# Projecting the eight sample tokens: contraction split, or output columns split, over TensorE's column groups

## The chip, the cores and the metric

One core of a Trainium2 chip runs the whole program. The metric is the device time of one execution in microseconds. TensorE (PE) multiplies, VectorE (DVE) and ScalarE (ACT) work elementwise and read PSUM, GpSimd (POOL) adds in SBUF, and SyncE (SP) issues most transfers. All data are fp32.

## The reference, cut to what matters

Two decoder layers over 512 prompt tokens and 8 sample tokens (one new token for each of 8 sequences). The part in question is the input projection, applied to both:

```python
def project_mixers(h, w_in_l, pos):          # h: rmsnorm(x, g_mix_pre[l]), 1024 wide
    z = h @ w_in_l
    qa, ka, va, qi, ki, wi, qb, kb, vb, gb = jnp.split(z, splits, axis=-1)
    ...                                      # rope on q, k, qi, ki
```

After it come a sparse attention (indexer scores, top-k, softmax over the selected keys), a retention mixer, an output product and a feed-forward block with squared ReLU.

## The kernel before

**Tiling.** The 520 tokens are five tiles: four of 128 prompt tokens (`NT` = 4) and tile 4 with the 8 sample tokens (`TILES` = 5, `NB` = 8). `w_in` is cut into eight chunks of columns, in the order indexer (324 columns, `W_IDX`), q, k, v of group A, q, k, gate, v of group B (512 each, `W`). `project(c, between)` (from L671) runs over the tiles of chunk `c`; the tile's number in the layer is n = 5c + i. For a prompt tile each of the eight contraction blocks k of 128 is one matmul (L690): 128 tokens stationary, 512 weight columns moving, added up in one PSUM bank. One fp32 matmul appears in the trace as two LDWEIGHTS and two MATMUL records.

**The sample tile before.** Eight tokens would fill 8 of the array's 128 columns. So the contraction is split: block k goes to the column group k // 2, that is to PSUM partitions 32(k // 2) and on (L694), with the last 32 tokens stationary, of which the last eight are wanted. The order of k is 0, 2, 4, 6, 1, 3, 5, 7, so that four column groups work side by side. Four partial sums then lie on four partition ranges. ScalarE copies the whole bank into `parts` (`take_parts`, L1155), and a matmul with the constant `addp` adds the four ranges up on partitions 0 to 7 of the same bank (`add_parts`, L649). TensorE issues that matmul after two blocks of the next tile. Then ScalarE scales and copies the result to SBUF (`evacuate`, L1182; in chunk 0 first the four columns of `wi`, L1178).

**What runs between.** `between(i, k)` is called after each block k and puts other work among the matmuls: transposes, indexer scores, and in chunks 4 (tile 3) to 6 the attention of 32 (block, head) steps (`attend`, steps listed by `head_steps`). A step's scores come from TensorE (L828), DVE masks them and takes the maximum (L1619, L1622), ScalarE exponentiates (L1221), DVE normalises (L1630), TensorE transposes (L838), ScalarE copies (L1216), TensorE multiplies with v (L815). Each engine has one order of work, written out by hand: ScalarE evacuates the tile before at the first step of a tile, and DVE ropes it (L1575 to L1581) or, for the gate, takes its sigmoid. Chunk 7 begins with the sample tile, with a group of transposes (L709) after every second block.

**Waits.** Two banks alternate (`proj_bank`, n % 2), so tile n waits until n - 2 is evacuated (`proj_read`, L680). In layer 0, chunk 0 is computed block by block for four prompt tiles in banks 0 to 3 (`first_chunk`, L659), after which TensorE waits for all constants (`const_in`, 13 loads on ScalarE's queue, the last is `addp`). The sample tile then uses bank 0 again. `token_sums`, `token_roots` and `token_scales` give each token's 1/rms, by which `evacuate` scales; for the sample tokens it is wanted on the partitions on which they are read. In layer 1 that runs inside chunk 0. SyncE's weight loads wait for `proj_done` of the chunk that used the ring slot.

Of the kernel before, what the change touches and what calls it, by code (L numbers as in the profile page):

```python
# [23 lines left out]
NB = 8  # L24
# [25 lines left out]
CONSTS = 13  # L50
# [14 lines left out]
def token_cols(t):  # L65
    return slice(t * P, t * P + rows(t))

# [119 lines left out]
def down_ready(q, which):  # L187
# [8 lines left out]
    proj_done=40, tok_mm=2, part_mm=8, tr_mm=19, ts_mm=3, dot_mm=12, sdot_mm=1, wm_mm=1, ssc_mm=1, cache_used=16,  # L196
    vrep_mm=1, spt_mm=1, att_mm=32, pt_mm=32, pv_mm=32, as_mm=1, ra_mm=8, su_mm=4, o_mm=4, bt_mm=5, mt_done=16,
    stat_mm=6, st_mm=168, tok_std=3, proj_read=40, part_read=8, tr_read=19, ts_read=3, dot_read=12, srelu_done=1,
# [42 lines left out]
def build(nc, x, w_idx, w_all, gains, g_first, g_ret, cache_k, cache_v, cache_ki, state, pages, tab_cos, tab_sin,  # L241
# [3 lines left out]
    with ctx:  # L245
# [95 lines left out]
        parts = sb("parts", [P, W]); addp = sb("addp", [P, NB]); dg = sb("dg", [P, NH]); ones = sb("ones", [P, P]); eps = sb("eps", [P, 1])  # L341
# [34 lines left out]
        part_mm = sem("part_mm")  # L376
        part_read = sem("part_read")
# [103 lines left out]
        def proj_bank(n):  # L481
            return n if now[0] == 0 and n < NT else n % 2
# [130 lines left out]
        def _(pe):  # L613
# [30 lines left out]
            def add_parts(n):  # L644

                c = n // TILES
                pe.wait_ge(part_read, past(part_read) + c + 1)
                width = W if c else W_IDX
                mm(ps[0:NB, proj_bank(n), 0:width], addp[:], parts[:, 0:width], start=True, stop=True).then_inc(proj_done, 1)  # L649
# [19 lines left out]
            def project(c, between):  # L669
                width = W if c else W_IDX  # L670
                for i, t in enumerate(tile_order(c)):  # L671
# [11 lines left out]
                    for j, k in enumerate(ks):  # L683
                        if i == 0 and j == (4 if t < NT else 2):
                            unit_here(2 * c + 1)
# [394 lines left out]
        def _(act):  # L1080
# [213 lines left out]
            for l in range(DEPTH):  # L1294
# [54 lines left out]
                for g in range(2):  # L1349
                    if g:  # L1350
                        take_parts(3)
# [887 lines left out]
```

## Time and profile before

| | |
|---|---|
| median of 3 runs | 1653.7 us (1651.63 to 1654.96) |
| the profiled execution | 1654.42 us, its span 1652.6 us |
| TensorE, matmul records | 1580.8 us, 96% of the span, 6986 records |
| TensorE, weight loads | 1101.5 us, 67% |
| DVE, ScalarE, GpSimd | 831.6 us (50%), 432.5 us (26%), 420.8 us (25%) |
| DMA | 150.26 MB, mean 91 GB/s |
| granted TensorE clock | 0.987 of 2.4 GHz, mean |

Layer 0 goes to about 824 us; the projection and its mixers take the stretch to about 365 us in layer 0, and 824 to about 1180 us in layer 1. The output products and the feed-forward block fill the rest. A matmul record counts as busy to its modelled end, also while the next one runs beside it, so a high share does not mean that the array works at its peak. Idle time stands beside a group with what ended it.

### The profile page before, as it was taken

How to read it: one execution, taken by the hardware profiler on the slowest of the kernel's cores; microseconds unless marked ns; L12 is line 12 of the kernel's file. 1: busy time of each engine (PE TensorE's matmuls, PEld its weight loads, DVE VectorE, ACT ScalarE, POOL GpSimd, SP SyncE). 2: the span in 40 equal slices, each digit the busy share in tenths (PEclk: the TensorE clock that was granted, in tenths of full speed). 3: DMA queues.
4: the chain of work that ended last, by engine and by line, in shares of the span. 5: the costliest groups of instructions: out<-in, count | busy, mean ns of one | idle time of the engine just before them, and what ended most of it. 6: DMA issues, size and time to landing. Idle time of an engine off the chain costs nothing.

```text
span 1652.6 us, 19575 instructions
## 1 busy us (share of the span) xinstructions
PE 1580.8 (96%) x6986; PEld 1101.5 (67%) x6986; DVE 831.6 (50%) x1761; ACT 432.5 (26%) x975; POOL 420.8 (25%) x332
## 2 busy tenths in 40 slices
PE   7999899999999999999989998999999999999995
PEld 4344344478888888888843433445888888888884
DVE  4498556684743002332566984577646420133335
ACT  4312244314422002210142212443244310032100
POOL 0000000113363433353420000010226433343451
PEclk9999999999999999999999999999999999999998
DMA  6135401121422122312123252101233312222211
GB/s 203 63 127 167 146 20 52 53 78 55 153 102 103 72 82 102 103 51 102 63 94 102 77 202 105 52 1 54 81 103 127 105 74 103 102 80 100 77 51 52
DMA packets 52498, 150.26 MB, mean 91 GB/s; under 512 B 8331, under 2 KB 29331, under 8 KB 39091
## 3 DMA queue, kind: packets, MB, share of 16 engines
q1 hardware_dynamic: 44770, 140.65, 24.3%
q10 hardware_dynamic: 7632, 8.36, 1.5%
q8 instruction: 56, 0.92, 0.2%
q14 instruction: 40, 0.32, 0.1%
HBM read 139.79 MB, written 9.02 MB: 90 GB/s over the span
## 4 chain that ended last, share of the span: by engine, by line
PE 76%; DVE 16%; ACT 3%; issue 2%; DMA 2%; SPq 1%; ACTq 0%; DVEq 0%; POOL 0%; POOLq 0%
PE ps L1028 42%; PE ps L690 17%; PE ps L966 7%; DVE arena L1604 1%; DVE x_feat L1753 1%; DVE top L1602 1%; DVE arena L1643 1%; PE ps L694 1%; PE ps L828 1%; ACT arena L1182 1%; DVE s_sb L1751 1%; PE ps L815 1%; PE ps L838 1%; PE ps L649 1%; PE ps L924 1%
## 5 line engine op out<-in xcount | busy, mean ns | idle before, releaser
L690 PE MATMUL ps<-wring,h_feat 128*128 128x512 f32 (+1 forms) x960 | 438.6, 596 | 4.2 <-ACT arena L1182 2.8
L690 PEld LDWEIGHTS ps<-wring,h_feat 128*128 128x128 f32 x960 | 173.3, 193 | 192.7 <-issue 181.2
L1028 PE MATMUL ps<-arena,wring 128*128 128x256 f32 (+1 forms) x1280 | 285.8, 382 | 0.3 <-DVE arena L1832 0.3
L1028 PEld LDWEIGHTS ps<-arena,wring 128*128 128x128 f32 x1280 | 243.1, 190 | 37.7 <-DVE arena L1832 1.1
L1028 PE MATMUL ps<-h_feat,wring 128*128 128x256 f32 (+1 forms) x768 | 176.8, 382 | 2.5 <-DVE arena L1832 2.5
L2086 POOL TENSOR_TENSOR wring<-wring,arena 128x512 f32<-128x512 f32 (+1 forms) x48 | 78.8, 1641 | 341.2 <-PE ps L1028 321.6
L1028 PEld LDWEIGHTS ps<-h_feat,wring 128*128 128x128 f32 x768 | 145.8, 190 | 24.8 <-DVE arena L1832 3.3
L1028 PE MATMUL ps<-mix,wring 128*128 128x256 f32 (+1 forms) x512 | 123.6, 391 | 3.9 <-DVE s_sb L1806 3.9
L1028 PE MATMUL ps<-arena 128*128 128x264 f32 x512 | 119.2, 386 | 0.0
L966 PE MATMUL ps<-mix,wring 128*128 128x256 f32 (+1 forms) x512 | 115.0, 383 | 0.8 <-ACT mix L1242 0.8
L1028 PEld LDWEIGHTS ps<-mix,wring 128*128 128x128 f32 x512 | 99.4, 194 | 20.9 <-DVE s_sb L1806 4.8
L2069 POOL TENSOR_TENSOR pt_sb<-pt_sb 128x256 f32<-128x256 f32 (+1 forms) x98 | 76.7, 783 | 130.7 <-ACT pt_sb L1114 127.7
L1028 PEld LDWEIGHTS ps<-arena 128*128 128x128 f32 x512 | 97.3, 190 | 16.4
L966 PEld LDWEIGHTS ps<-mix,wring 128*128 128x128 f32 x512 | 96.5, 190 | 15.5 <-issue 1.2
L1182 ACT ACTIVATE arena<-ps,rtok 128x512 f32<-128x512 f32 (+3 forms) x80 | 53.2, 665 | 201.1 <-PE ps L690 173.0
L2110 POOL TENSOR_TENSOR arena<-arena,gret 128x512 f32<-128x512 f32 (+1 forms) x10 | 14.6, 1458 | 320.6 <-ACT arena L1189 320.6
L2086 POOL TENSOR_TENSOR arena<-wring 128x512 f32<-128x512 f32 (+1 forms) x48 | 79.0, 1646 | 50.5 <-DMA wring<-in_w_all 33.1
L1283 ACT ACTIVATE arena<-arena 128x264 f32<-128x264 f32 (+1 forms) x96 | 40.4, 421 | 192.4 <-DVE arena L1832 143.5
L2086 POOL TENSOR_TENSOR wring<-wring 128x512 f32<-128x512 f32 (+1 forms) x48 | 79.0, 1645 | 3.8
L2086 POOL TENSOR_TENSOR arena<-arena,wring 128x512 f32<-128x512 f32 (+1 forms) x48 | 78.9, 1643 | 3.8
L2104 POOL COPY arena<-kTs 128x4 f32<-128x4 f32 x16 | 3.1, 191 | 245.9 <-ACT kTs L1343 229.1
L1028 PE MATMUL ps<-h_feat,arena 128*128 128x264 f32 x256 | 62.2, 386 | 0.0
(212 smaller groups left out, 1800.8 us busy)
## 6 DMA issues: line engine op xcount, KB each, us to landing
wring<-in_w_all SPq DMA_DIRECT2D x108, 1024.0 KB, 5.0
arena<-in_cache_k SPq DMA_DIRECT2D x32, 256.0 KB, 5.3
arena<-in_cache_v SPq DMA_DIRECT2D x32, 256.0 KB, 4.3
wring<-in_w_idx SPq DMA_DIRECT2D x4, 648.0 KB, 5.6
x_feat<-in_x SPq DMA_DIRECT2D x4, 520.0 KB, 6.4
o_k_out<-arena ACTq DMA_DIRECT2D x2, 1024.0 KB
o_v_out<-arena ACTq DMA_DIRECT2D x2, 1024.0 KB
arena<-in_state SPq DMA_DIRECT2D x2, 1024.0 KB, 4.9
```

What stands on the lines that cost most here:

```text
L649: mm(ps[0:NB, proj_bank(n), 0:width], addp[:], parts[:, 0:width], start=True, stop=True).then_inc(proj_done, 1)
L690: last = mm(ps[:, proj_bank(n), 0:width], h_feat[:, k, token_cols(t)], wt, start=(k == 0), stop=(k == KD - 1))
L694: last = mm(ps[q4:q4 + 32, proj_bank(n), 0:width], h_feat[:, k, TOK - 32:TOK], wt, start=(k % 2 == 0), stop=(k % 2 == 1))
L815: last = mm(ps[e * HD:(e + 1) * HD, 6 + b % 2, (h // 2) * P:(h // 2 + 1) * P], v_tok[:, m, (h + e) * HD:(h + e + 1) * HD], pt_sb[e][:, m * ...
L828: mm(ps[:, 4 + e, 0:(b + 1) * P], qT[rr, h // 2, b * P:(b + 1) * P], kT[rr, h // 2, 0:(b + 1) * P], start=True, stop=True).then_inc(att_mm, 1)
L838: last = nc.tensor.transpose(ps[:, 2 + j % 2, m * P:(m + 1) * P], p_sb[j % 2][:, m * P:(m + 1) * P], idn[:])
L966: last = mm(ps[:, item_bank(n), 0:span(h)], wring[u % SLOTS][:, (m % 2 * KD + k) * P:(m % 2 * KD + k + 1) * P], mix[:, k, HALVES[h]], star ...
L1028: last = mm(out, a[:, j, :], b, start=(opens(n) and j == 0), stop=(j == nk - 1), skip_group_check=True)
L1182: nc.scalar.activation(dst, src, ACT.Copy, scale=rtok[0:r, sc, t:t + 1]).then_inc(proj_read, 1)
L1283: nc.scalar.activation(f, f, ACT.Relu).then_inc(act_step, 1)
L2069: nc.gpsimd.tensor_tensor(ssum[:, hc], ssum[:, hc], sqr[added % 2][:, 0:span(h)], ALU.add).then_inc(sq_used, 1)
L2086: nc.gpsimd.tensor_tensor(dst, in0, in1, op).then_inc(s_ready, 1)
```

## The change

The sample tile's output columns, not its contraction, are spread over the column groups. For each block k four matmuls, one per group g, multiply the same 8 tokens (stationary, 8 columns) with a quarter of the weight columns (128; in chunk 0 80, 80, 80 and 84). Group g's result lies complete on partitions 32g to 32g + 7. There are 32 small matmuls per tile in place of 8, in the plain order of k. `take_parts`, `add_parts`, their two semaphores, the tensors `parts` and `addp` and the load of `addp` go. `evacuate` reads the four pieces one after another from their partitions and joins them in SBUF; in chunk 0 the last is preceded by `wi`. The scales of the sample tokens are computed on four partition ranges: `token_sums(1)` makes four small matmuls for them and `token_roots(1)` four roots. In layer 0, the sample tile of chunk 0 gets bank 4 and waits for no evacuation, and the two tiles after it wait for two.

```diff
+def sample_cols(c):
+    cuts = (0, 80, 160, 240, W_IDX) if c == 0 else (0, P, 2 * P, 3 * P, W)
+    return list(zip(cuts[:-1], cuts[1:]))
...
         def proj_bank(n):
-            return n if now[0] == 0 and n < NT else n % 2
+            return n if now[0] == 0 and n < TILES else n % 2
+        def bank_taken(n):
+            if now[0] == 0 and n < TILES:
+                return None
+            return past(proj_read) + (2 if now[0] == 0 and n in (TILES, TILES + 1) else n - 1)
...
             def token_sums(h):
-                for t in ((0, 1), (2, 3, NT))[h]:
-                    last = mm(ps[0:rows(t), 6 + h, t:t + 1], ssum[:, token_cols(t)], ones[:, 0:1], start=True, stop=True)
+                for t in ((0, 1), (2, 3))[h]:
+                    last = mm(ps[:, 6 + h, t:t + 1], ssum[:, token_cols(t)], ones[:, 0:1], start=True, stop=True)
+                for q4 in range(0, P if h else 0, 32):
+                    last = mm(ps[q4:q4 + NB, 6 + h, NT:TILES], ssum[:, SEQ:TOK], ones[:, 0:1], start=True, stop=True)
...
-                    if n == NT and now[0] == 0:
-                        pe.wait_ge(proj_read, 1)
-                    elif n >= 2:
-                        pe.wait_ge(proj_read, past(proj_read) + n - 1)
-                    ks = range(KD) if t < NT else (0, 2, 4, 6, 1, 3, 5, 7)
+                    if n >= 2 and bank_taken(n):
+                        pe.wait_ge(proj_read, bank_taken(n))
...
                         else:
-                            q4 = 32 * (k // 2)
-                            last = mm(ps[q4:q4 + 32, proj_bank(n), 0:width], h_feat[:, k, TOK - 32:TOK], wt,
-                                      start=(k % 2 == 0), stop=(k % 2 == 1))
-                        if j == 1 and n and (i == 0 or tile_order(c)[i - 1] == NT):
-                            add_parts(n - 1)
+                            for g, (c0, c1) in enumerate(sample_cols(c)):
+                                last = mm(ps[32 * g:32 * g + NB, proj_bank(n), 0:c1 - c0], h_feat[:, k, SEQ:TOK], wt[:, c0:c1],
+                                          start=(k == 0), stop=(k == KD - 1))
...
+                    for q4 in range(0, P, 32):
+                        rr = slice(q4, q4 + NB)
+                        nc.scalar.activation(std_tok[rr, NT:TILES], ps[rr, 7, NT:TILES], ACT.Sqrt, bias=eps[rr]).then_inc(tok_std, 1)
...
-                if t == NT and counts.get(part_read.num, 0) == past(part_read) + c:
-                    take_parts(c)
...
+                pieces = sample_cols(c) if t == NT else [(0, W if c else W_IDX)]
+                for g, (c0, c1) in enumerate(pieces):
+                    rr, end = slice(32 * g, 32 * g + r), (W if c else W_IDX - NI)
+                    if c1 > end:
...
+                    done = proj_read if g == len(pieces) - 1 else act_step
+                    nc.scalar.activation(dst[:, c0:c1], ps[rr, proj_bank(n), 0:c1 - c0], ACT.Copy,
+                                         scale=rtok[rr, sc, t:t + 1]).then_inc(done, 1)
+                    act.wait_ge(done, up(done))
```

## Rows read from the trace of the kernel before

**Rows 1.** The profile page, chain that ended last, shares by engine.

```profile
PE 76%; DVE 16%; ACT 3%; issue 2%; DMA 2%; SPq 1%; ACTq 0%; DVEq 0%; POOL 0%; POOLq 0%
```

**Rows 2.** Busy time by stretch: PE, PEld, DVE, ACT, POOL (instructions), clock, DMA share, GB/s.

```profile
45.60:189.00 143.40, 137.91 (x487) 56.55 (x486) 104.22 (x249) 30.80 (x58) 1.53 (x8) 0.99 0.38 126
189.00:311.00 122.00, 112.17 (x536) 50.31 (x536) 78.03 (x211) 52.81 (x125) 7.29 (x5) 0.99 0.13 47
```

**Rows 3.** Groups by form, whole span: count, busy us, mean ns, idle before.

```profile
L694 PE MATMUL ps<-wring,h_feat 128*32 128x512 f32 x224 | 32.7, 602 | 0.0
L649 PE MATMUL ps<-parts,addp 128*8 128x512 f32 x28 | 14.6, 604 | 9.9 <-ACT parts L1155 9.9
...
L1182 ACT ACTIVATE arena<-ps,rtok 8x512 f32<-8x512 f32 x14 | 9.5, 677 | 14.5 <-PE ps L649 14.3
L1155 ACT ACTIVATE parts<-ps 128x512 f32<-128x512 f32 x14 | 8.4, 597 | 5.2 <-PE ps L694 4.9
...
L1216 ACT ACTIVATE pt_sb<-ps 128x128 f32<-128x128 f32 x16 | 4.4, 277 | 18.8 <-PE ps L838 17.8 <-ACT p_sb L1221 0.9
```

**Rows 4.** Small passes, loads and two waits of TensorE's sequencer: timeline, groups, lines.

```profile
280.24 1.09 PE L815 MATMUL ps<-pt_sb,arena 128*64 128x128 f32 x16
...
136.88 1.95 PE L797 MATMUL ps<-arena,qs 128*32 128x257 f32 x32
...
193.67 0.16 PEld L694 LDWEIGHTS ps<-wring,h_feat 128*32 128x32 f32 x8
...
L649 PEld LDWEIGHTS ps<-parts,addp 128*8 128x8 f32 x32 | 1.7, 87 | 22.1 <-ACT parts L1155 16.8 <-issue 5.3
...
L792 PEldq EVENT_SEMAPHORE  x1: 51/51/51, 150.7 to 150.7; - x1
...
L680 PEldq EVENT_SEMAPHORE  x1: 51/51/51, 151.3 to 151.3; - x1
```

**Rows 5.** Timeline of the start of layer 0: start, length, what, idle before and releaser.

```profile
29.02 1.28 ACT L1130 ACT_TABLE_LOAD   x1 [13.93 <-DMA addp<-in_sum_parts]
...
32.28 2.39 PE L694 MATMUL ps<-wring,h_feat 128*32 128x324 f32 x16 [4.19 <-ACT arena L1182]
...
32.46 0.53 ACT L1182 ACTIVATE arena<-ps,rtok 128x320 f32<-128x320 f32 x1
...
40.53 0.48 DVE L1581 TENSOR_TENSOR arena<-arena,rstd_ffn 8x320 f32<-8x320 f32 x1
...
43.14 1.04 PE L709 MATMUL ps<-idn,arena 128*128 128x128 f32 x8
```

**Rows 6.** Timeline at the change from chunk 4 to chunk 5, layer 0.

```profile
199.80 0.29 DVE L1630 TENSOR_SCALAR p_sb<-p_sb,rinv 128x128 f32<-128x128 f32 x1
...
200.84 1.03 PE L649 MATMUL ps<-parts,addp 128*8 128x512 f32 x2 [2.08 <-ACT parts L1155]
...
204.74 0.68 DVE L1575 TENSOR_TENSOR arena<-arena,cosT 8x512 f32<-8x512 f32 x1 [3.60 <-ACT arena L1182]
```

**Rows 7.** Chunk 5 to 6, layer 0: timeline, and the stretch behind the adding matmul.

```profile
249.62 1.03 PE L649 MATMUL ps<-parts,addp 128*8 128x512 f32 x2 [2.61 <-ACT parts L1155]
...
250.60:252.50 1.90, 1.90 (x5) 0.40 (x4) 0.00 (x0) 0.00 (x0) 0.00 (x0) 0.53 0.40 78
...
255.07 0.56 DVE L1619 CUSTOM_DVE_ANT_0 s_sb<-ps,arena 128x384 f32<-128x384 f32 x1 [6.28 <-PE ps L828]
```

**Rows 8.** Timeline of the first tile of chunk 7, layer 0.

```profile
306.70 1.05 PE L694 MATMUL ps<-wring,h_feat 128*32 128x512 f32 x4
...
308.28 1.23 ACT L1203 ACTIVATE arena<-ps 128x512 f32<-128x512 f32 x2
```

**Rows 9.** Timeline of layer 1: the token scales in chunk 0, and chunk 3's adding matmul.

```profile
848.05 0.24 ACT L1133 ACTIVATE std_tok<-ps,eps 8x1 f32<-8x1 f32 x1
849.15 0.26 ACT L1178 ACTIVATE wi<-ps,rtok 128x4 f32<-128x4 f32 x1 [0.85 <-PE ps L690]
...
969.61 1.02 PE L649 MATMUL ps<-parts,addp 128*8 128x512 f32 x2 [0.49 <-ACT parts L1155]
```

More of the change, by code:

```diff
@@ L49 @@
 CHUNKS = 8
-CONSTS = 13
+CONSTS = 12
 FT = 16
@@ L340, in build @@
         idn = sb("idn", [P, P]); exps = sb("exps", [NB, 2, P]); sel = sb("sel", [P, 2, NB])
-        parts = sb("parts", [P, W]); addp = sb("addp", [P, NB]); dg = sb("dg", [P, NH]); ones = sb("ones", [P, P]); eps = sb("eps", [P, 1])
+        dg = sb("dg", [P, NH]); ones = sb("ones", [P, P]); eps = sb("eps", [P, 1])
         pg = sb("pg", [1, NB * NPAGES], I32)
@@ L676, in project @@
                         unit_here(2 * c)
-                    if n == NT and now[0] == 0:
-                        pe.wait_ge(proj_read, 1)
-                    elif n >= 2:
-                        pe.wait_ge(proj_read, past(proj_read) + n - 1)
-                    ks = range(KD) if t < NT else (0, 2, 4, 6, 1, 3, 5, 7)
-                    for j, k in enumerate(ks):
-                        if i == 0 and j == (4 if t < NT else 2):
+                    if n >= 2 and bank_taken(n):
+                        pe.wait_ge(proj_read, bank_taken(n))
+                    for k in range(KD):
+                        if i == 0 and k == 4:
                             unit_here(2 * c + 1)
@@ L692, in project @@
                         else:
-                            q4 = 32 * (k // 2)
-                            last = mm(ps[q4:q4 + 32, proj_bank(n), 0:width], h_feat[:, k, TOK - 32:TOK], wt,
-                                      start=(k % 2 == 0), stop=(k % 2 == 1))
-                        if j == 1 and n and (i == 0 or tile_order(c)[i - 1] == NT):
-                            add_parts(n - 1)
-                        if j < KD - 1:
-                            between(i, j)
-                    last.then_inc(proj_done if t < NT else part_mm, 1)
+                            for g, (c0, c1) in enumerate(sample_cols(c)):
+                                last = mm(ps[32 * g:32 * g + NB, proj_bank(n), 0:c1 - c0], h_feat[:, k, SEQ:TOK], wt[:, c0:c1],
+                                          start=(k == 0), stop=(k == KD - 1))
+                        if k < KD - 1:
+                            between(i, k)
+                    last.then_inc(proj_done, 1)
                     between(i, KD - 1)
@@ L1094, in _ @@
                      (causal_bias[:], causal), (sel[:], select), (dg[:], diag), (dm[:], dmask), (kdec[:], k_decay),
-                     (qdec[:], q_decay), (cdec[:], c_decay), (gam[:], s_gamma), (addp[:], sum_parts)]
+                     (qdec[:], q_decay), (cdec[:], c_decay), (gam[:], s_gamma)]
             assert len(loads) == CONSTS
@@ L1149, in normed @@
                 square(norm, h, k, x_feat[:, k, HALVES[h]])
-            def take_parts(c):
-                n, width = c * TILES + tile_order(c).index(NT), W if c else W_IDX
-                act.wait_ge(part_mm, past(part_mm) + c + 1)
-                nc.scalar.activation(parts[:, 0:width], ps[:, proj_bank(n), 0:width], ACT.Copy).then_inc(part_read, 1)
-                act.wait_ge(part_read, up(part_read))
             def evacuate(c, i):
@@ L1383, in _ @@
                 take_groups([qT[:, h, :] for h in range(4)])
-                take_parts(7)
                 take_groups([kT[:, h, :] for h in range(4)])
@@ L1856, in token_scales @@
             def token_scales(h):
-                dve.wait_ge(tok_std, past(tok_std) + (3 if h else 1))
+                dve.wait_ge(tok_std, past(tok_std) + (6 if h else 1))
                 ts = slice(2, TILES) if h else slice(0, 2)
```

26 lines of the change are left out of this document (5 added, 21 removed).

## Prediction

> **What bounds the kernel now.** I read the chain of waits first, then the busy time by stage, then the groups by form, then the order of events around each adding matmul. The chain [rows 1] lies on TensorE for 76% of the span, VectorE for 16% and ScalarE for 3%: what TensorE issues, and what it waits for, sets the end. The stages differ [rows 2]. In chunks 1 to 4 (45.6 to 189 us) TensorE is busy for 137.9 of 143.4 us; in the attention stretch (189 to 311) for 112.2 of 122, with the other engines far from full, so three engines hand work around and the missing 10 us are waits. The product and feed-forward stages behind are not touched.
>
> The profiled execution took 1654.4 us, of which the span is 1652.6. The median is 1653.7, so I make the sum against 1654.4 and take nothing off for the 0.7.
>
> **Sample tiles.** One fp32 matmul shows as two MATMUL records, "passes". Before, a sample tile is 16 passes of 512 columns. 224 such records fill 32.7 us although each lasts 0.60 [rows 3], so four column groups run beside each other, and a tile is four rounds, about 1.85 us. After, it is 64 passes of 128 columns on the same four groups, the same columns per group: 16 rounds of four passes. How long is a round? Two-group matmuls of 128 columns put 16 passes, eight rounds of two, into 1.09 us [rows 4]. That holds the drain of the last; without a drain of some 0.2 a round is 0.11 us, a quarter of the 0.43 that a round of 512 columns takes: the columns alone. Sixteen rounds give 1.75 us: as long as before, within 0.1. Two things could make a round longer. The weight loads: a load of 8 columns is recorded with 87 ns, but eight loads of 32 columns at 193.67 lie within 0.16 us [rows 4], each 0.11 long, so they start some 7 ns apart and overlap. And the sequencer: after a blocked wait at 150.7 (L792) it reaches the wait behind sixteen such matmuls (L680) at 151.3 [rows 4], 0.6 us for 32 passes and 32 loads, under 40 ns a matmul; the new tile needs one per 54 ns. I take 0.03 us more per tile, 0.5 us in all; the bounds are 0 and what the first rival costs.
>
> The Trainium skill ("TensorE: Matmul & The Clock Gate", Part 1) says that with hardware decode off the sequencer spends about 62 ns per MATMUL. By that rule 64 passes last 3.97 us a tile and the sum below would come out at about 1661 us; the 32 passes in 0.6 us speak against it here, though they are the only such place I found.
>
> **Adding matmuls.** They go: 28 records of 512 columns in 14.6 us and 9.9 us of idle in front of them [rows 3], 0.955 us of TensorE each from start to next start, 0.64 in chunk 0. TensorE is the bound in chunks 1 to 3, so three times 0.955 = 2.9 us come back in each layer. DVE is full from 79 to 151 us, but it starts that run on the sample tile's evacuation, which also comes earlier, so it keeps pace. In chunk 3 of layer 1 there is also 0.49 us of idle in front [rows 9]: 0.4 more.
>
> **Evacuation.** ScalarE lost a copy of 0.60 us per tile and now makes four pieces in place of one of 0.68 [rows 3]. A 128-column copy takes 0.28 [rows 3], with a semaphore step about 0.31, so four pieces are 1.2 to 1.3 us: 0.6 more on the way from the tile's last matmul to the rope, against 1.6 (copy, adding matmul) taken out of it. Where DVE or TensorE waits for that rope this 0.6 counts, and it is in the terms below. Elsewhere ScalarE waits for TensorE and hides it. If that cover were gone everywhere it would cost 16 x 0.6 = 10 us. SyncE's weight loads wait for the end of a chunk's last tile, which comes earlier; no queue is moved past another.
>
> **Start of layer 0.** The sample tile waited for bank 0 until 32.28 (4.19 idle) and the stage's transposes began at 43.14 [rows 5]. Now the tile has bank 4 and can run as soon as the constants are in (29.0), and the next tile waits for two evacuations (33.0) [rows 5] where it waited for four. It ends at about 40, 16 passes of 0.43 later; its transposes then wait for the last rope, L1581 ending at 41.0 [rows 5], which does not move: ropes are late next. That is 2.1 us, and 0.3 more since ScalarE, which evacuated tile 5 before it took the transposes' first group, has done so by then: 2.4. ScalarE's first work, at 29.02, was released by the DMA of addp, the last constant [rows 5]; without it that comes between 0 and 1 us earlier (TensorE's own first stage ends at 28.1); I take 0.3. Together 2.7 (0.6 to 3.7).
>
> **Chunk 4 to 5.** TensorE stood 2.08 us for the copied parts at 200.84, before 0.955 us of adding [rows 6]: 3.0 at most. But the next steps hang on DVE, which idled 3.60 us until the sample tile was evacuated and started its rope at 204.74 [rows 6]. Without the adding matmul ScalarE still has step 5's copy and exponential behind DVE's L1630 of 199.80; they end near 201.4, four pieces end near 202.7, the rope starts at 202.8. So 2.0 (0.96 to 3.0) per layer.
>
> **Chunk 5 to 6.** The same with 2.61 us of wait [rows 7], and worse: the two passes behind it fill 1.9 us at a granted clock of 0.53 in that stretch (near the 1.2 GHz level), after the engine had stood, against 0.86 at the full one. Step 20's score matmuls stood behind all that, and DVE idled 6.28 us for them [rows 7]. So TensorE gains 2.6, 0.95 and 1.0 for the clock up to step 20, and 0.6 in that step, which ran half slow too: 5.2. DVE's rope of the sample tile gains the same less the 0.6 of the pieces: 4.6. DVE and TensorE wait for each other by turns behind it; I take 5.0 (0.96 to 5.2) per layer.
>
> **Chunk 6 to 7.** Two adding matmuls, 1.9 us. Also, chunk 7 begins with the sample tile, cut by transposes after each two k; of the four column groups such a pair used two, and its four passes took 1.05 us with the drain [rows 8], 0.98 to the next start. Now a pair of k fills all four groups: four rounds, 0.44. Four times 0.54 gives 2.2. But the third transpose group waits until ScalarE has taken the first, which it began at 308.28 [rows 8]; without the wait for the adding matmul, and with the pieces, that is near 307.1, its end 307.7, and TensorE is there at 306.8: it stands 1.0 us where it stood none. Net 1.9 + 2.2 - 1.0 = 3.1 (1.9 to 4.1).
>
> **Layer 1, chunk 0.** The adding matmul gives 0.64. The deviation of the sample tokens is now wanted on four partition ranges: four small matmuls, and three more ScalarE roots of 0.24 [rows 9] that overlap a little, in front of the scales for which L1178 at 849.15 waits [rows 9]. That is 0.65 later. Net 0 (-0.3 to 0.3).
>
> **Sum.** Layer 0: 2.7 + 2.9 + 2.0 + 5.0 + 3.1 = 15.7. Layer 1: 0 + 3.3 + 2.0 + 5.0 + 3.1 = 13.4. Less 0.5 for the tiles: 28.6. 1654.4 - 28.6 = 1625.8, say **1626 us**; with the terms' bounds 1618 to 1634.
>
> **Rivals.** First, *the small passes do not fit in a round*. If the 1.95 us that 32 passes of 257 columns took [rows 4] is a rate of 60 ns a pass rather than their columns, a tile lasts 3.84 us, 2.1 more, sixteen times 33.6: 1626 + 33.6 = 1659 us, slower. At the recorded 87 ns of an 8-column load [rows 4], 5.57 us a tile, it would be near 1685. It decides from 1.8 us more per tile, 55 ns a pass, on. For it: these passes come one in some 54 to 60 ns and I found no long stretch with faster ones, and that is break-even. Against: in all of them the columns explain that number, and the loads and the sequencer go faster [rows 4]. Chance 0.12.
>
> Second, *the attention stretch keeps its length*: softmax steps on DVE and ScalarE take the place of the waits for the copied parts. Then the 14 us of chunk 4 to 6 shrink to about 2: 1638 to 1640. For it: DVE's steps form a chain there and DVE starts at once where it can. Against: its idle of 3.60 and 6.28 us sits exactly behind these waits. Chance 0.2.
>
> Third, *partial gain*: rounds of 0.14 us in place of 0.11 (0.5 us a tile) and a longer evacuation, 1634. Chance 0.08. The forecast has 0.6.
>
> **Range.** 1618 to 1643: forecast, third and second rival and their edges; only the first lies outside. A difference of 0.2%, 3.3 us, is about what a measurement of this kernel can tell from none. Only the first rival reaches that side: faster 0.87, same 0.05 (a first rival at break-even), slower 0.08.
>
> **What would show it.** Sample tile of chunk 1: start to next start near 1.8 us (first rival: over 3). No idle over 1 us at the two places where it was 2.08 and 2.61; the rope of the sample tile of chunk 4 some 2 us, the scores of step 20 some 5 us nearer to the tile before them. Start: transposes near 41.0. Chunk 7: pairs of k at 0.44 to 0.5. If tiles stay at 1.8 and the gain is small, the prediction fails in the attention stretch; if they are long, in the round.

## The result and the profile after

The kernel after takes 1628.4 us (median of 4 runs, 1627.58 to 1632.61) against 1652.66 us for the kernel before beside it (4 runs, 1651.55 to 1654.96): a ratio of 0.9857, 95% interval 0.9836 to 0.9878. Measured again on another chip it was 1628.85 against 1653.92, ratio 0.9850 (0.9835 to 0.9864). The forecast was 1626, the range 1618 to 1643. Where a gain stands below with an interval, both are worked out from the ratio; the difference of the medians can be 1.6 us off it.

First the page of the profiled run (1627.84 us, span 1626.1): busy time, and the chain that ended last by engine, to be read against [rows 1].

```profile
PE 1557.1 (96%) x7734; PEld 1116.2 (69%) x7734; DVE 832.8 (51%) x1761; ACT 438.3 (27%) x1013; POOL 421.4 (26%) x332
...
PE 69%; DVE 20%; ACT 5%; issue 3%; DMA 2%; POOL 1%; SPq 0%; ACTq 0%; DVEq 0%; POOLq 0%
```

TensorE's share of the chain fell from 76% to 69%, VectorE's rose from 16% to 20% and ScalarE's from 3% to 5%. The hand-overs between engines weigh more now; that is where the rest of this document finds what was mis-sized.

The groups of TensorE by form (busy us, mean ns, idle in front), which answer to [rows 3], then ScalarE's:

```profile
L696 PE MATMUL ps<-wring,h_feat 128*8 128x128 f32 x896 | 29.3, 273 | 0.0
...
L1178 ACT ACTIVATE arena<-ps,rtok 8x128 f32<-8x128 f32 x56 | 20.2, 361 | 6.3 <-PE ps L696 4.6
```

896 small passes fill 29.3 us. A piece of the evacuation takes 361 ns, where the forecast had 0.28 from a plain copy of 128 columns [rows 3].

The timeline of TensorE around the sample tile of chunk 1, layer 0 (start, length, what):

```profile
72.73 1.94 PE L696 MATMUL ps<-wring,h_feat 128*8 128x128 f32 x64
74.59 1.98 PE L692 MATMUL ps<-wring,h_feat 128*128 128x512 f32 x4
```

From start to next start it is 1.86 us for 64 passes. The tile is as long as before, and no adding matmul cuts the next one. That saves more than the adding matmul's 0.955 us: before, the next tile's first eight passes took 1.92 us ahead of the cut (75.48 to 77.40) and 1.92 behind it (78.35 to 80.27); uncut they take 3.64 (74.59 to 78.23), 0.2 less.

The start of layer 0, TensorE and ScalarE, which answers to [rows 5]:

```profile
29.21 1.82 PE L696 MATMUL ps<-wring,h_feat 128*8 128x80 f32 x64 [2.47 <-DMA gam<-in_s_gamma]
33.75 8.59 PE L692 MATMUL ps<-wring,h_feat 128*128 128x512 f32 x16 [2.72 <-ACT arena L1178]
42.18 1.04 PE L709 MATMUL ps<-idn,arena 128*128 128x128 f32 x8
...
29.23 1.28 ACT L1130 ACT_TABLE_LOAD   x1 [14.51 <-DMA gam<-in_s_gamma]
...
30.83 1.07 ACT L1135 ACTIVATE std_tok<-ps,eps 8x1 f32<-8x1 f32 x4
```

And the granted clock there (window, length, busy by engine, PEclk, DMA share, GB/s):

```profile
33.00:36.00 3.00, 2.25 (x3) 1.17 (x4) 2.76 (x8) 2.16 (x6) 0.00 (x0) 0.50 1.00 421
36.00:42.00 6.00, 6.00 (x14) 2.57 (x13) 5.38 (x14) 1.55 (x5) 0.00 (x0) 0.94 0.27 115
```

Chunk 4 to 5 of layer 0 ([rows 6] before), TensorE, then VectorE's rope of the sample tile and ScalarE's pieces:

```profile
199.15 2.10 PE L883 MATMUL ps<-sel,arena 128*128 128x8 f32 x16
201.11 3.39 PE L692 MATMUL ps<-wring,h_feat 128*128 128x512 f32 x4
...
195.59 0.68 DVE L1567 TENSOR_TENSOR arena<-arena,cosT 8x512 f32<-8x512 f32 x1 [1.91 <-ACT arena L1178]
...
193.96 1.54 ACT L1178 ACTIVATE arena<-ps,rtok 8x128 f32<-8x128 f32 x4
```

Chunk 5 to 6 ([rows 7] before) and chunk 7 ([rows 8]):

```profile
237.57 2.81 PE L692 MATMUL ps<-wring,h_feat 128*128 128x512 f32 x6 [0.52 <-ACT arena L1178]
240.32 0.88 PE L815 MATMUL ps<-pt_sb,arena 128*64 128x128 f32 x12
...
292.18 0.62 PE L696 MATMUL ps<-wring,h_feat 128*8 128x128 f32 x16
292.74 0.66 PE L709 MATMUL ps<-idn,arena 128*128 128x128 f32 x4
...
295.86 0.66 PE L709 MATMUL ps<-idn,arena 128*128 128x128 f32 x4 [0.77 <-ACT arena L1200]
```

Where the stall of 2.61 us was, 0.52 is left. A pair of k of chunk 7 takes 0.56 us to the next start.

Chunk 3 of layer 1 ([rows 9] has its adding matmul), TensorE, then ScalarE:

```profile
953.22 2.06 PE L852 MATMUL ps<-arena,exps 8*128 8x512 f32 x4 [0.77 <-ACT arena L1178]
955.21 5.24 PE L692 MATMUL ps<-wring,h_feat 128*128 128x512 f32 x8
...
949.04 1.28 ACT L1348 ACT_TABLE_LOAD   x1 [4.83 <-DVE nms L1909]
...
951.53 1.54 ACT L1178 ACTIVATE arena<-ps,rtok 8x128 f32<-8x128 f32 x4
```

To see where the time went, take the start of the same matmul in both traces. This table is worked out from them (us; "gain" is before less after; tuned2 is a kernel of the last experiment):

```
same matmul                                    before    after   gain   tuned2
first transposes of layer 0                     43.14    42.18    1.0    42.17
2nd tile of chunk 2, layer 0                    85.08    83.04    2.0    82.75
2nd tile of chunk 3, layer 0                   119.14   115.95    3.2   115.66
scores of the cache (L870), layer 0            182.82   175.09    7.7   174.20
step behind chunk 4 to 5 (L828), layer 0       212.29   204.80    7.5   201.14
step behind chunk 5 to 6, 2nd tile             262.01   249.88   12.1   245.44
behind chunk 7 (L894), layer 0                 319.42   304.49   14.9   299.88
chunk 0 of layer 1, 1st tile                   828.81   812.64   16.2   808.24
2nd tile of chunk 1, layer 1                   901.00   883.76   17.2   879.55
2nd tile of chunk 2, layer 1                   935.05   916.67   18.4   912.74
2nd tile of chunk 4, layer 1                   997.51   980.12   17.4   975.88
step behind chunk 4 to 5, layer 1             1025.13  1006.01   19.1  1000.96
step behind chunk 5 to 6, layer 1             1074.85  1051.08   23.8  1045.26
behind chunk 7's groups, layer 1              1128.73  1102.15   26.6  1096.15
```

Each column is one profiled run, so single places carry chance. A second profiled run of the kernel after (on the other chip) has 4.7 in place of 7.7 at L870 of layer 0 and 25.4 in place of 26.6 in the last row; between the rows behind chunk 4 to 5 and those behind chunk 5 to 6 it has the same 4.7 in both layers.

### The profile page after: what moved, and what is told of

Read it like the earlier page. It is cut to its first block, busy times and chain, and to the rows that moved or that the text cites. A ratio compares the mean times of both kernels' runs of the same rounds, so it can differ in the third digit from the quotient of the medians.

```text
span 1626.1 us, 21092 instructions
## 1 busy us (share of the span) xinstructions
PE 1557.1 (96%) x7734; PEld 1116.2 (69%) x7734; DVE 832.8 (51%) x1761; ACT 438.3 (27%) x1013; POOL 421.4 (26%) x332
## 4 chain that ended last, share of the span: by engine, by line
PE 69%; DVE 20%; ACT 5%; issue 3%; DMA 2%; POOL 1%; SPq 0%; ACTq 0%; DVEq 0%; POOLq 0%
PE ps L1028 43%; PE ps L692 12%; PE ps L966 6%; DVE arena L1596 3%; DVE top L1594 3%; ACT arena L1178 2%; DVE x_feat L1745 1%; DVE arena L1635 1%; DVE arena L1567 1%; DVE arena L1573 1%; PE ps L828 1%; DVE s_sb L1743 1%; DVE s_sb L1611 1%; PE ps L924 1%; PE ps L838 1%
## 5 line engine op out<-in xcount | busy, mean ns | idle before, releaser
L692 PE MATMUL ps<-wring,h_feat 128*128 128x512 f32 (+1 forms) x960 | 436.2, 595 | 7.5 <-ACT arena L1178 6.0
L692 PEld LDWEIGHTS ps<-wring,h_feat 128*128 128x128 f32 x960 | 174.9, 193 | 188.6 <-issue 176.4
L1178 ACT ACTIVATE arena<-ps,rtok 128x512 f32<-128x512 f32 (+3 forms) x128 | 65.5, 512 | 194.2 <-PE ps L692 185.2
L1028 PE MATMUL ps<-mix,arena 128*128 128x264 f32 x256 | 62.2, 386 | 0.0
```

The source lines that it names most:

```text
L692: last = mm(ps[:, proj_bank(n), 0:width], h_feat[:, k, token_cols(t)], wt, start=(k == 0), stop=(k == KD - 1))
L1028: last = mm(out, a[:, j, :], b, start=(opens(n) and j == 0), stop=(j == nk - 1), skip_group_check=True)
L1178: nc.scalar.activation(dst[:, c0:c1], ps[rr, proj_bank(n), 0:c1 - c0], ACT.Copy, scale=rtok[rr, sc, t:t + 1]).then_inc(done, 1)
```

## Experiments

The times of before are 1653.07 us (20 runs) beside the three parts alone and the part undone; 1652.4 (13) beside the cut passes, the one piece, the later adding matmul and the first tuning; 1653.92 (9) beside the last two kernels; and 1652.67 (9) beside the one of chunks 4 and 5 with the later adding matmul.

**One part alone: chunks 4 and 5 (run cols45).** In this and the next two kernels the copy and the adding matmul stay for the chunks named.

```diff
+CONTRACTED = (0, 1, 2, 3, 6, 7)
...
+                    whole = t < NT or c not in CONTRACTED
...
+                        elif not whole:
+                            q4 = 32 * (k // 2)
+                            last = mm(ps[q4:q4 + 32, proj_bank(n), 0:width], h_feat[:, k, TOK - 32:TOK], wt,
...
+                            if tile_order(pc)[pi] == NT and pc in CONTRACTED:
+                                add_parts(n - 1)
```

> The kernel before, with the sample tile split by columns in chunks 4 and 5 alone; the other six chunks keep contraction parts, copy and adding matmul. Theory (the waits for the copied parts are what costs, as the forecast had it): 2.0 + 5.0 us per layer, 14.0 in all, so 1638.6; going by where the kernel after gained, 0.2 to 1.7 us at chunk 4 to 5 and 4.6 at chunk 5 to 6 in each layer, it is 11 us, about 1641.5. Rival (only the adding matmuls count, other waits of the attention stretch take the place of the two stalls): 4 x 0.955 = 3.8 us, about 1649.

Measured: 1644.07 us, ratio 0.9936 (0.9915 to 0.9957), 10.6 us less with an interval of 7 to 14. (The medians differ by 9.0.) By the rows of the table above, the trace gives 4.6 us at chunk 5 to 6 in both layers. Chunk 4 to 5 gains 1.7 us up to L883 in both layers and gives 1.6 back on the way to the step behind, in slow passes. The rival of 3.8 us falls. The same trace gains 2.6 us in chunk 3 of layer 0, where this kernel changes nothing: so much can come and go there by chance.

**One part alone: chunks 1 to 3 (run cols123).** `CONTRACTED = (0, 4, 5, 6, 7)`.

> The kernel before, with the split by columns in chunks 1, 2 and 3 alone. Theory (TensorE is the bound there): 2.9 us in layer 0 and 3.3 in layer 1 by the forecast, about 1646.5. By the trace of the kernel after, 1.15 us per chunk in chunks 1 and 2 of each layer, 1 to 3 in chunk 3 of layer 0, where the transfers of the cache end the wait, and a loss of up to 0.8 in chunk 3 of layer 1: 5.5 to 7.5 us, 1645 to 1647. Rival (VectorE, which is full behind chunk 1, keeps the length): under 2 us, 1651 or more.

Measured: 1648.73 us, 0.9970 (0.9954 to 0.9986): 5.0 us less, interval 2.3 to 7.6. In layer 1 the three chunks gain 1.14, 1.14 and 0.96 us in the trace. TensorE is the bound there, and a chunk gives 1.15, not 0.955: the adding matmul and the 0.2 of the cut. TensorE's row at the end of chunk 3, layer 1:

```profile
965.33 1.95 PE L871 MATMUL ps<-arena,exps 8*128 8x512 f32 x4 [0.64 <-ACT arena L1208]
967.21 3.70 PE L703 MATMUL ps<-wring,h_feat 128*128 128x512 f32 x8
```

Nearly the stall of the kernel after (0.77), but the eight passes behind it take 3.70 us and not 5.24. So of what chunk 3 of layer 1 lost in the kernel after, 1.5 us is clock, not the change's order.

This kernel also has the old order at chunk 5 to 6, with the old stall, and happens to keep its clock there:

```profile
247.74 1.02 PE L664 MATMUL ps<-parts,addp 128*8 128x512 f32 x2 [2.61 <-ACT parts L1178]
248.70 1.12 PE L703 MATMUL ps<-wring,h_feat 128*128 128x512 f32 x2
```

The two passes behind it take 1.05 us to the next start where the kernel before took 1.90 [rows 7], and the place is 1.6 us shorter in both layers with nothing changed in it. So of what a kernel without slow passes saves there against the profiled run of before, 1.6 us is clock. The slow passes of this run lie at chunk 4 to 5 of layer 0 instead, which is 2.0 us longer, also unchanged.

**One part alone: chunk 7 (run cols7).** `CONTRACTED = (0, 1, 2, 3, 4, 5, 6)`.

> The kernel before, with the split by columns in chunk 7 alone, where the sample tile comes first and is cut by transposes after each two k. Theory: the adding matmul of chunk 7 goes (0.955), a pair of k goes from 0.98 to 0.55 us to the next start (four times 0.43 = 1.7), and the third group of transposes stands up to 0.8 us for ScalarE: 1.9 to 2.7 us per layer, about 1648.5 in all. Rival (only the adding matmul counts, and the pairs of k are hidden behind ScalarE's taking of the groups): 2 x 0.955 less the wait, 1652 or so.

Measured: 1649.23 us, 0.9980 (0.9970 to 0.9991): 3.3 us less, interval 1.5 to 5.0. The trace gives 1.9 us per layer in chunk 7, in two parts: 0.8 up to the first full tile and 1.1 at the transposes behind it. The theory holds, the rival (1652) lies outside.

The three parts alone sum to 10.6 + 5.0 + 3.3 = 18.9 us of the 24.3. Chunks 0 and 6 were not run alone; the trace of the kernel after has about 1 us for the start and 0.9 per layer for chunk 6's adding matmul (2.8 at chunk 6 to 7, less the 1.9 of chunk 7), and the rest is within the scatter of the clock.

**One part undone: the bank and the early tile (run bank0).**

```diff
-            return n if now[0] == 0 and n < TILES else n % 2
+            return n if now[0] == 0 and n < NT else n % 2
-            return past(proj_read) + (2 if now[0] == 0 and n in (TILES, TILES + 1) else n - 1)
+            return past(proj_read) + n - 1
```

> The kernel after, with one part undone: in layer 0 the sample tile of chunk 0 again goes to bank 0 and waits for the first evacuation, and the next tile waits for four. The forecast's term for the early tile was 2.4 us (2.7 with the constants): then this kernel is 2.4 us slower than the kernel after, 1630.8. Theory from the trace of the kernel after, where chunk 1's first tile starts early only to run 8.6 us at a low granted clock: the early tile brings 0.5 us or less, 1628 to 1629, and chunk 1's first tile runs at a higher granted clock than in the kernel after.

Measured: 1632.01 us, 0.9868 (0.9844 to 0.9892), 3.6 us over the kernel after; the intervals overlap. The profiled run is 8.8 us longer than after's in its span, and its mean granted clock is 0.984 against 0.989. Two stretches of it:

```profile
34.73 9.65 PE L692 MATMUL ps<-wring,h_feat 128*128 128x512 f32 x16 [1.31 <-ACT arena L1178]
...
156.00:163.00 7.00, 7.00 (x10) 2.66 (x9) 6.69 (x14) 1.20 (x2) 0.00 (x0) 0.52 1.04 394
```

My expectation that the tile behind would run at a higher clock fell: it takes 9.65 us. The times alone hardly tell what the bank is worth: two of the four runs, at a clock of 0.989, took 1629.7 and 1630.3, 0.7 to 2.4 us more than the kernel after at that clock. The traces tell more. Counted from the last constant (28.27 here, 29.23 in the kernel after), chunk 1's first tile starts after 6.46 us here and after 4.52 in the kernel after, and 4.51 to 4.52 in three more profiled runs with bank 4 (the second of the kernel after, the cut passes, the one piece). That is 1.9 us for the early tile, so the theory's 0.5 falls. The first transposes follow after 15.9 us here and 13.0 to 14.5 in those four, so the forecast's 2.4 is in reach; the tile between runs through the slow clock in each of them and adds the scatter.

**The price of a pass (run halves).** Each sample matmul of 128 columns cut in two.

```diff
-                            for g, (c0, c1) in enumerate(sample_cols(c)):
+                            for part in range(2 if c else 1):
+                                for g, (c0, c1) in enumerate(sample_cols(c)):
+                                    h0, h1 = (part * (P // 2), (part + 1) * (P // 2)) if c else (0, c1 - c0)
```

> The kernel after, with each sample matmul of 128 columns in chunks 1 to 7 cut into two of 64 (128 passes a tile in place of 64, the same columns; chunk 0 as it was). Theory (the columns set the tile, what the sequencer and the weight loads need per pass lies under them): no change, 1628 us, and a tile of 1.9 us from start to next start. First rival of the forecast (a pass costs what it costs, whatever its columns), with its price lowered to the 29 ns a pass that the kernel after shows at most (64 passes in 1.86 us): 1.86 us more per tile, 14 tiles, 26 us more, 1654. Anything between tells the true price of a pass.

Measured: 1630.7 us, 0.9873 (0.9850 to 0.9896). TensorE in chunk 1:

```profile
72.32 1.97 PE L698 MATMUL ps<-wring,h_feat 128*8 128x64 f32 x128
74.22 1.98 PE L692 MATMUL ps<-wring,h_feat 128*128 128x512 f32 x4
```

128 passes from start to next start in 1.90 us, 15 ns a pass; the tile grew by 0.04. The columns set the tile, and the first rival is out by far. (This kernel leaves something out: the sample rows of chunks 1 to 7 are not the full sums. Both halves start in one bank, and the later start seems to make the first half lose its first k, which was not tried by itself. The work issued is as described.)

**The price of four pieces (run one_piece).**

```diff
-                pieces = sample_cols(c) if t == NT else [(0, W if c else W_IDX)]
+                pieces = sample_cols(c) if t == NT and c == 0 else [(0, W if c else W_IDX)]
```

> The kernel after, with the sample tile of chunks 1 to 7 evacuated by one ScalarE copy of 512 columns from the first partition range, as in the kernel before. It leaves out three of the four pieces of these tiles (what is copied is right in the first 128 columns alone). Theory: four pieces take 1.54 us where one takes 0.68, and this counts where VectorE or TensorE waits for the evacuation: at chunk 4 to 5 and 5 to 6 of each layer about 0.8 us each, at chunk 3 of layer 1 up to 0.8, in chunk 7 up to 0.8 per layer: 3 to 5 us less than the kernel after, 1624 to 1625. Rival (ScalarE is hidden everywhere): no change, 1628.

Measured: 1616.71 us, 0.9791 (0.9774 to 0.9808), 11.7 us under the kernel after, two to four times what the theory had. The same place as above, ScalarE, VectorE and TensorE:

```profile
193.27 0.68 ACT L1178 ACTIVATE arena<-ps,rtok 8x512 f32<-8x512 f32 x1
...
194.05 0.68 DVE L1567 TENSOR_TENSOR arena<-arena,cosT 8x512 f32<-8x512 f32 x1 [1.04 <-ACT arena L1178]
...
199.35 1.96 PE L692 MATMUL ps<-wring,h_feat 128*128 128x512 f32 x4
```

Four pieces take 1.54, one takes 0.68: the difference of 0.86 appears whole at each of eight places, at chunk 3, 4 to 5, 5 to 6 and 6 to 7 of both layers (by the starts of the same matmuls 0.8 to 1.1 each; 0.7 of it is given back in layer 0 at the cache's transfers). That is some 7 us. The rest is the clock: `L692` x4 takes 1.96 in place of 3.39, chunk 3 of layer 1 has no stall and no slow passes behind it (2.5 us in all), and the mean clock of the four runs is 0.991 to 0.993, that of the nine runs of the kernel after 0.987 to 0.990.

**The place of the adding matmul (run late3).** The kernel before, one number changed.

```diff
-                        if j == 1 and n and (i == 0 or tile_order(c)[i - 1] == NT):
+                        if j == 3 and n and (i == 0 or tile_order(c)[i - 1] == NT):
```

> The kernel before, with the adding matmul issued after the fourth k of the next tile in place of the second, 0.86 us later in the order of TensorE. The two stalls of TensorE, 2.08 and 2.61 us, shrink by that to 1.2 and 1.7, while the copied parts and so the evacuation and the rope come no earlier. Theory (in the attention stretch the way copy, adding matmul, evacuation, rope sets the time, TensorE's own standing little): within 1 us of the kernel before. Rival (what TensorE stands is lost one for one): 4 x 0.86 = 3.4 us less, 1649.6.

Measured: 1647.46 us, 0.9971 (0.9959 to 0.9983), 4.8 us less (2.8 to 6.8). My theory fell, and the rival is too small at the decisive place. By the trace this kernel gains 4.3 us at chunk 5 to 6 in both layers, nearly the 4.6 of the kernel after, and 1.4 at chunk 4 to 5. It gives back 1.7 us in chunk 3 of layer 0 and 4.8 in layer 1, there 3.0 of it in slow passes. TensorE at chunk 5 to 6:

```profile
244.85 2.81 PE L690 MATMUL ps<-wring,h_feat 128*128 128x512 f32 x6 [0.52 <-ACT arena L1182]
247.60 0.88 PE L815 MATMUL ps<-pt_sb,arena 128*64 128x128 f32 x12
248.40 0.92 PE L828 MATMUL ps<-arena 64*128 64x384 f32 x4
...
250.59 1.02 PE L649 MATMUL ps<-parts,addp 128*8 128x512 f32 x2
```

The head step's matmuls (L815, L828) need nothing of the copied parts. Before, they stood behind the blocked adding matmul; here they run first, and when the adding matmul comes its parts are ready. It costs 0.95 and no stall. Of the 4.3 us, 2.7 are the stall and 1.6 the clock, which was low behind the stall in both layers of the profiled run of before (see the run of chunks 1 to 3).

**The place alone, where it helps (run late45).** The same edit for chunks 4 and 5 only.

```diff
-                        if j == 1 and n and (i == 0 or tile_order(c)[i - 1] == NT):
+                        if j == (3 if c in (5, 6) else 1) and n and (i == 0 or tile_order(c)[i - 1] == NT):
```

> The kernel before, contraction parts, copies and adding matmuls all kept; only the adding matmuls of chunks 4 and 5 are issued two k of the next tile later, behind the head step's matmuls, as in the run late3, and those of the other chunks stay where they were. Theory (what costs at chunk 4 to 5 and 5 to 6 is that TensorE waits for the copied parts in front of a head step that does not need them, the matmul itself counts 0.955 at most): by the places in late3 1.4 + 4.6 us per layer, some 12 us less the 1 to 1.5 us that come back in chunk 7: 1642 to 1645, as much as the split by columns in the same two chunks gave (1644). Rival (only taking out copy and adding matmul brings it; what late3 showed there was the clock): 1649 or more.

Measured: 1640.62 us, 0.9921 (0.9907 to 0.9936), 13.1 us less (10.6 to 15.4), against 10.6 (7 to 14) for the split by columns in the same two chunks. The trace has the same 1.4 and 4.3 us per layer as late3, 11.3 in all, and nothing back in chunk 7. The split by columns has 1.7 and 4.6 there where no slow pass takes it back, so the two edits are within 0.6 us per layer of each other, and the lead of 2.5 us of this one lies in the clock (0.991 to 0.992 against 0.988 to 0.991). So most of what these chunks had to give does not hang on taking the adding matmul out. It hangs on what stands behind it in TensorE's queue, and one changed line brings it.

**A first tuning of the new costs (run tuned).**

```diff
                     token_roots(0)
-                    token_roots(1)
                     for i in range(2):
                         evacuate(0, i)
+                    token_roots(1)
...
-                    nc.scalar.activation(std_tok[:, 2:NT], ps[:, 7, 2:NT], ACT.Sqrt, bias=eps[:]).then_inc(tok_std, 1)
-                    for q4 in range(0, P, 32):
+                    nc.scalar.activation(std_tok[:, 2:TILES], ps[:, 7, 2:TILES], ACT.Sqrt, bias=eps[:]).then_inc(tok_std, 1)
...
+                    if g >= len(pieces) - 2:
+                        act.wait_ge(done, count)
```

> The kernel after, with three edits where its trace shows the new costs. In layer 0 ScalarE evacuates the first two tiles ahead of the second set of roots (as layer 1 does); the deviations of the third and fourth tile and of the sample tokens are one root over all partitions in place of five, with one matmul that fills the rows between the samples; ScalarE no longer waits after each of the four pieces, only ahead of the last. Theory: the next tile of chunk 1 in layer 0 starts near 32 in place of 33.75 and the ropes 1 us earlier, 1.0 us; four roots are 0.7 to 0.8 us of ScalarE in layer 1 too, of which up to 0.6 counts; four pieces take 1.3 us in place of 1.54, which counts at five or six places with 0.2: 2 to 3 us less than the kernel after, 1625.5. Rival (these waits are hidden, or the granted clock takes it back): 1628.

Measured: 1628.87 us, 0.9870 (0.9851 to 0.9889), nothing gained. The next tile started at 32.5 in place of 33.75, but ran through the same slow clock, and the first transposes came at 41.96 in place of 42.18; four pieces took 1.52 in place of 1.54, so the waits between them had cost next to nothing. The ropes came no earlier either: the second set of scales now stands behind two ropes in VectorE's order, ScalarE waited 3.10 us for it, and the last rope ended at 41.91 in place of 41.61. The mean clock of these runs was 0.9875. The rival was right.

**The kernel after once more (run after2), and a version with the eight places mended (run tuned2).** The edits of tuned2 beside those of the start:

```diff
+                if t == NT and c in SHARED:
+                    dve.wait_ge(proj_done, past(proj_done) + n + 1)
+                    for g, (c0, c1) in list(enumerate(sample_cols(c)))[2:]:
+                        v.tensor_scalar(raw[(j * TILES + t) % 3][0:NB, c0:c1], ps[rr, proj_bank(n), 0:c1 - c0],
...
                 for g in range(2):
+                    if g:
+                        evacuate(3, 4)
...
-                evacuate(6, TILES - 1)
                 block_out(NT - 1)
-                take_groups([qT[:, h, :] for h in range(4)])
+                take_groups([qT[:, h, :] for h in range(2)])
+                evacuate(6, TILES - 1)
+                take_groups([qT[:, h, :] for h in range(2, 4)])
```

> The kernel after once more, beside tuned2 on the same chip. Both theories: 1628 us, within 3.

> The kernel after, with edits at the four places where the run with one piece gained: (1) chunks 4 and 5: VectorE, which waits there, takes the third and fourth piece of the sample tile while ScalarE takes the first two; (2) chunk 3: ScalarE evacuates the sample tile between its two softmax exponentials in place of behind both; (3) chunk 6: ScalarE writes the last attention output and takes the first two groups of transposes ahead of the sample tile's pieces; (4) the start as in the tuned kernel: roots in one, two evacuations ahead of the second set. All the work is there. Theory (the four pieces lie on the way of VectorE and TensorE at these places): 0.7 to 0.8 us each at chunk 3, 4 to 5, 5 to 6 and 6 to 7 of both layers, about 6 us, and one or two stretches of low granted clock less, 1.5 us each: 1620 to 1622. Rival (the run with one piece gained by what it leaves out of the rows' data or by the clock alone): 1626 or more.

Measured: the kernel after 1628.85 us, 0.9850 (0.9835 to 0.9864); tuned2 1618.06 us, 0.9787 (0.9773 to 0.9800), 10.8 us under it, with all the work in. VectorE and ScalarE share the pieces at chunk 4 to 5, and chunk 3 of layer 1 has no stall:

```profile
192.54 0.73 DVE L1573 TENSOR_SCALAR arena<-ps,rtok 8x128 f32<-8x128 f32 x2
193.63 0.68 DVE L1585 TENSOR_TENSOR arena<-arena,cosT 8x512 f32<-8x512 f32 x1 [0.35 <-ACT arena L1183]
...
192.78 0.75 ACT L1183 ACTIVATE arena<-ps,rtok 8x128 f32<-8x128 f32 x2
...
948.47 1.98 PE L858 MATMUL ps<-arena,exps 8*128 8x512 f32 x4
950.38 3.70 PE L698 MATMUL ps<-wring,h_feat 128*128 128x512 f32 x8
```

The rival falls. By the starts of the same matmuls the places give 0.35 us at chunk 3 of layer 0 and 0.8 to 1.05 at each of the other seven, 6.4 in all, as the theory had it; the rest of the 10.8 goes with the clock (mean 0.991 to 0.993, the kernel after 0.987 to 0.990). It is the fastest kernel here that does the whole work. It was not run without the edits at the start; by the run before they bring nothing.

## Why the prediction was right

The sum was 28.6 us; the profiled run is 26.6 shorter (1654.4 to 1627.8), the median 24.3. The mechanism was right, and the near agreement also hides errors that cancel. Part of it is luck: the start and the evacuation were sized wrong, and in the one trace of before chunk 3 of layer 0 and a later stage ran slow by chance, which made up for it. The terms' bounds, all low or all high, give 1620 to 1641 by their own numbers, not 1618 to 1634.

- **Tile, 0.03 more, at most 3.84 us.** It is 1.86 against 1.85: right. The weight loads and the sequencer are not near a bound, as the cut passes show. The Trainium skill's 62 ns per MATMUL with hardware decode off ("TensorE: Matmul & The Clock Gate", Part 1) is not what these runs show, and no run tells whether hardware decode is off in them: 64 passes in 1.86 us are 29 ns each, 128 in 1.90 are 15, and counted by the matmul, two passes each, 58 and 30.
- **Adding matmuls, 0.955 each.** 1.15 in chunks 1 and 2 of both layers: 0.2 per chunk too low.
- **Chunk 3.** In layer 0 the gain grows by 3.4 us up to 159.10 (table's times of before) where the sum had 1.0, and by 1.1 more up to L870. Of the 3.4, 1.1 is the adding matmul with its cut. 1.4 is the wait for the cache's transfer in front of L797, which ended at 150.80 before and 146.23 after, 4.6 us earlier where TensorE was 3.2 ahead. SyncE's transfers may come earlier with the chunk's end, which I had taken as hidden; but against the same trace of before, cols45, cols7 and late45, which change nothing in chunk 3, gain 0.5, 1.4 and 0.8 at this wait, so at most half of the 1.4 can be put down to the change. 1.5 is clock and not the change's: before ran slow behind that wait (granted clock 0.73 from 150.8 to 157.2), after did not (1.00 from 146.2 to 152.4). And 0.6 is lost at a stall of 0.67 in front of L852, the four pieces' doing (with one piece it is not lost). The 1.1 behind it is the second cache transfer, for which TensorE waits 0.80 us in place of 1.89. The first two lines are before, the others after:

```profile
150.80 2.81 PE L797 MATMUL ps<-arena,qs 128*32 128x257 f32 x32 [2.43 <-DMA arena<-in_cache_k]
153.54 2.76 PE L690 MATMUL ps<-wring,h_feat 128*128 128x512 f32 x4
...
146.23 1.95 PE L797 MATMUL ps<-arena,qs 128*32 128x257 f32 x32 [1.03 <-DMA arena<-in_cache_k]
148.11 3.70 PE L692 MATMUL ps<-wring,h_feat 128*128 128x512 f32 x8
```

In the second profiled run of the kernel after, the slow passes lie behind L852, the second wait is 1.74, and the chunk gives 1.9 us up to L870, not 4.5. In layer 1 it lost 1.0 in place of gaining 1.4: a stall of 0.77, since the pieces stand behind two exponentials that wait for VectorE, and 1.5 us of slow passes behind it. In cols123, with nearly the same stall and no slow passes, the chunk gained 0.96.
- **Start, 2.7.** 1.0 was gained, 0.6 in the second profiled run. The constants did not come earlier in this pair (the last transfer ended the wait at 29.2, before at 29.0); over all profiled runs they are in at 28.9 on average with addp (6 runs, 28.3 to 29.3) and at 28.5 without (7 runs, 28.1 to 29.2), so the 0.3 may be right. Two steps failed. The four roots, 1.07 us, which I counted in layer 1 alone, stand in front of the first evacuation here too: the second evacuation ends at 33.6, the next tile starts at 33.75, not 33.0, and the last rope ends at 41.6, not 41.0. And that tile takes 8.59 us, not 6.9, at a granted clock of 0.50 in its first stretch.
- **Chunk 4 to 5, 2.0.** 1.7 in layer 1, -0.2 in layer 0, where `L883` and the tile behind it ran slow: 3.39 us for four passes that take 1.96. In the second profiled run, without slow passes there, it is 1.5 and 1.7. The pieces took 1.54, not 1.2 to 1.3.
- **Chunk 5 to 6, 5.0.** 4.6 and 4.7: right in size. As to its cause, the forecast had said that step 20's scores stood behind the adding matmul; late3 and late45 show that this place in the queue alone gives 4.3. The adding matmul itself gives about 1 more and the four pieces take 0.86 of it back: with one piece it is 5.4.
- **Chunk 6 to 7, 3.1.** 2.8 in both layers. Pairs of k 0.56 in place of 0.44, the third group's stall 0.77 in place of 1.0.
- **Layer 1, chunk 0.** -0.1 against 0: right.
- **The rivals.** The first falls by the tile. The second, that the attention stretch keeps its length, falls too: from L870 to L894 of layer 0 the gain grows from 7.7 to 14.9 us. The third had the longer evacuation right but not the longer rounds.
- **Not in the sum.** 1.3 us appear in layer 0 between L894 and layer 1, in stages that the change does not touch: the profiled run of before had a stretch of low clock there (`450:460` at 0.83), that of after none. It is chance, and made up for part of what the start and chunk 3 of layer 1 lacked.
- **The evacuation, 0.6 per tile.** The term that was sized worst. I had it at 0.6, in the terms of the three places in each layer, and hidden elsewhere. It is 0.86, counts at four places in each layer (7 us in the trace), and goes with a lower clock: 11.7 us between four pieces and one. With one piece's price the gain would have been 36 us, not 24.

## What to carry to other kernels

Look at what stands behind a blocked instruction in its engine's queue before you take the instruction out: here a later place for two matmuls per layer gave 13 us without any change of the data layout. When an output is split over partition ranges, count the evacuation by pieces at the measured time of that very form (with its scale), ask at each place which engine waits for it, and give pieces to the engine that waits. Sum the profile's gain by the starts of the same instructions in both traces, and take out stretches of low clock first.

## What the runs showed of the hardware

- **The length of a run goes with its mean granted clock.** In 20 runs of the kernel before the one at 0.986 took 1656.2 us, the three at 0.990 to 0.991 1649.0 to 1649.5; a line through them gives 1.3 us for 0.001. The low level comes behind waits of TensorE (0.70 from 29.2 to 31.0 behind 2.47 us of idle and 0.50 from there to 36; 953 to 960 behind 0.77), but not behind each. After 0.67 us of idle at 152.48 the clock stayed up, in a second run of the same kernel it was 0.57 from 154.6 to 158.6 behind the same wait (0.64), and in cols123 it stayed up behind 0.64 at 965.33 and 2.61 at 247.74. Some low stretches lie in times of heavy transfers (421 GB/s at 33 to 36; 394 at 156 to 163 in bank0), others in times of none (`201.10:204.40`, below). What decides it stays open.

```profile
201.10:204.40 3.30, 3.30 (x5) 1.16 (x5) 0.00 (x0) 0.00 (x0) 0.00 (x0) 0.56 0.00 0
...
953.00:960.00 7.00, 6.78 (x12) 2.88 (x13) 6.62 (x16) 1.27 (x3) 0.00 (x0) 0.76 1.02 375
```

- **Small passes on four column groups cost their columns alone down to 64 columns** (15 ns a pass with its weight load of 8 columns, recorded with some 90 ns: the loads overlap).
- **A ScalarE piece of 8x128 with a scale per partition takes 361 ns, one of 8x512 680 ns**, VectorE's of 8x128 out of the same bank 365. By these two the fixed part is about 0.25 us (an estimate), so four pieces cost more than twice one.
- **Two starts in one bank.** With the columns of a bank started in two halves, the sample rows came out short. The k and v of the sample tokens are off by 0.30 of their size over both layers. The loss of one of eight k in half of the columns would be 0.25 in the first layer (the square root of 1/8 x 1/2), and the second layer starts from wrong values; this is argued, not tried by itself.
